# Moving the split activation u by 96 bytes in SBUF in a two-block transformer kernel

## The reference, cut to what matters

```python
def modulate(x, g, shift, scale):
    return rmsnorm(x, g) * (1 + scale) + shift
x = x + 0.5 * m[:, 2] * swiglu(modulate(x, norm_g[i, 0], m[:, 0], m[:, 1]), w_gate, w_up, w_down)
...
h = rmsnorm_2(x, pre_norm[layer])
proj = h @ w_in[layer]
```

## Time and profile before

| | |
|---|---|
| time, median of 3 runs | 2276.56 us (2274.78 to 2280.75) |
| span of the profiled execution, first to last instruction (its own time; nothing around it is given) | 2276.9 us |
| TensorE (PE) matmuls busy | 2135.6 us, 94% |
| weight loads (PEld), beside the matmuls | 2025.3 us, 89% |
| VectorE (DVE) | 1453.4 us, 64% |
| ScalarE (ACT) | 963.4 us, 42% |
| mean granted TensorE clock | 0.941 of full |

### The profile page before, as it was taken

How to read it: one execution, slowest core, us unless ns; L and a number is a source line. 1 busy time by engine, 2 the same in 40 slices (tenths; PEclk the granted TensorE clock), 3 DMA queues, 4 the chain that set the end, 5 groups by cost and what they waited for, 6 DMA issues and landing times.

```text
span 2276.9 us, 38695 instructions
## 1 busy us (share of the span) xinstructions
PE 2135.6 (94%) x16399; PEld 2025.3 (89%) x16399; DVE 1453.4 (64%) x1820; ACT 963.4 (42%) x1091; POOL 174.4 (8%) x153
## 2 busy tenths in 40 slices
PE   5999999999979899999999999999998898899897
PEld 4999999987749799999999899999998698899767
DVE  3546777779789957777644644557755445775543
ACT  2433433334325644334333533445445345534532
POOL 1000000000010000000000000003300000330000
PEclk9999999999989799999999899999998889999878
DMA  9688688733233348886655355544434034443401
GB/s 322 241 276 277 222 275 295 269 105 119 74 93 121 107 143 278 277 293 224 208 186 180 109 188 186 182 133 149 131 113 130 8 123 145 138 127 112 130 1 56
DMA packets 270793, 383.86 MB, mean 169 GB/s; under 512 B 8441, under 2 KB 230727, under 8 KB 270679
## 3 DMA queue, kind: packets, MB, share of 16 engines
q1 hardware_dynamic: 246983, 293.59, 40.1%
q0 software_dynamic: 22288, 85.02, 10.7%
q10 hardware_dynamic: 1408, 3.59, 0.4%
HBM read 381.06 MB, written 1.11 MB: 168 GB/s over the span
## 4 chain that ended last, share of the span: by engine, by line
PE 80%; DVE 13%; ACT 4%; issue 3%; DMA 0%; SPq 0%; DVEq 0%; ACTq 0%
PE bank L635 21%; PE bank L636 21%; PE bank L637 21%; PE bank L1081 3%; DVE w_hl L1764 3%; PE bank L661 2%; ACT w_hl L1319 1%; DVE e_long L2143 1%; DVE e_long L2161 1%; PE bank L696 1%; DVE conv_acc L2092 1%; PE bank L681 1%; PE bank L708 1%; PE bank L1128 1%; ACT p_tile L1660 1%
## 5 line engine op out<-in xcount | busy, mean ns | idle before, releaser
L1764 DVE TENSOR_TENSOR w_hl<-raw,w_hl 128x2048 fp32r<-128x2048 f32 (+1 forms) x281 | 641.7, 2284 | 434.5 <-ACT w_hl L1319 434.2
L1319 ACT ACTIVATE w_hl<-raw 128x2048 fp32r<-128x2048 f32 (+1 forms) x281 | 532.3, 1894 | 223.7 <-PE bank L637 218.9
L635 PE MATMUL bank<-u_hl,w_hl 128*128 128x256 f32 x2080 | 596.1, 287 | 0.0
L636 PE MATMUL bank<-u_hl,w_hl 128*128 128x256 f32 x2080 | 591.9, 285 | 0.0
L637 PE MATMUL bank<-u_hl,w_hl 128*128 128x256 f32 x2080 | 591.7, 284 | 0.0
L635 PEld LDWEIGHTS bank<-u_hl,w_hl 128*128 128x128 f32 x2080 | 402.6, 194 | 10.1 <-issue 8.4
L636 PEld LDWEIGHTS bank<-u_hl,w_hl 128*128 128x128 f32 x2080 | 402.6, 194 | 0.0
L637 PEld LDWEIGHTS bank<-u_hl,w_hl 128*128 128x128 f32 x2080 | 402.4, 193 | 0.0
L635 PE MATMUL bank<-h_hi,w_hl 128*128 128x256 f32 x800 | 226.8, 284 | 3.8 <-DVE h_lo L1861 3.8
L636 PE MATMUL bank<-h_lo,w_hl 128*128 128x256 f32 x800 | 225.8, 282 | 0.0
L637 PE MATMUL bank<-h_hi,w_hl 128*128 128x256 f32 x800 | 225.5, 282 | 0.0
(11 more groups left out here) (395 smaller groups left out, 4108.2 us busy)
## 6 DMA issues: line engine op xcount, KB each, us to landing
ada<-in_ada_w POOLq DMA_DIRECT2D x72, 1024.0 KB, 7.0
raw<-in_w_in SPq DMA_DIRECT2D x60, 1024.0 KB, 5.2
raw<-in_ffn_w_gate SPq DMA_DIRECT2D x55, 1024.0 KB, 7.2
raw<-in_ffn_w_up SPq DMA_DIRECT2D x55, 1024.0 KB, 5.3
raw<-in_ffn_w_down SPq DMA_DIRECT2D x55, 1024.0 KB, 5.0
raw<-in_ssd_w_in SPq DMA_DIRECT2D x20, 1024.0 KB, 5.3
raw<-in_w_out SPq DMA_DIRECT2D x16, 1024.0 KB, 5.2
raw<-in_ssd_w_out SPq DMA_DIRECT2D x8, 1024.0 KB, 5.1
```

The source lines that it names most:

```text
L635: pe.matmul(out_, wh, xh, start=start, stop=False, skip_group_check=True)
L636: pe.matmul(out_, wh, xl, start=False, stop=False, skip_group_check=True)
L1319: nc.scalar.activation(whi[slot][:, 0:n], raw[slot][:, 0:n], ACT.Copy).then_inc(S["hi_done"], 1)
L1764: ve.tensor_tensor(wlo[slot][:, 0:n], raw[slot][:, 0:n], whi[slot][:, 0:n].bitcast(F32), ALU.subtract)\
```

## The change

`u_hl` begins 96 bytes later, at byte 98,528, which is 96 past a multiple of 128 (and 224 past one of 256). A further 32 bytes behind it make the whole shift 128 bytes for all that follows: `scratch` is on a multiple of 128 as before, `region` is 136,416, still 96 past a multiple of 128. What overlays u (`ada[6]`, `ada[7]`, `fin_hi`, `streams`) takes its address from `u_at` and moves by 96 too; the second half of `streams` is worked out from `region` and stays on `uc_hl`. No instruction is added, removed or moved.

```diff
         x = fixed("x", [P, KB, T])
+        top[0] += 96
         u_at = top[0]
         u_hl = fixed("u_hl", [P, 2, KB, T], F32R)
+        top[0] += 32
         u_hi, u_lo = u_hl[:, 0, :, :], u_hl[:, 1, :, :]
         scratch_at = top[0]
         scratch = fixed("scratch", [P, KB, T])
```

## The result

The change made the kernel slower: 2286.11 us (median of 6 runs, 2282.93 to 2288.83) against 2276.53 us (6 runs), 9.6 us or 0.42% by the medians; the ratio over the runs is 1.003 with a 95% interval of 1.0016 to 1.0045. The profiled run took 2286.14 us, 1.6 us more than its span. Forecast were 2266.0 us and a range from 2262.5 to 2277.0.

What follows compares the result with a forecast made beforehand. The prediction took TensorE's distance between matmul starts to bound the kernel; 10.0 + 0.3 + 0.5 + 0.4 + 0.2 - 0.2 - 0.6 = 10.6 us off 2276.6 gave 2266.0 us, range 2262.5 to 2277.

Steps and rivals of the forecast that it cites:

- What bounds the kernel: FFN stages with u moving: TensorE never idles, so stage time is matmul count times the distance between two starts.
- The distance and what it goes with: Matmul starts: 120.0 ns with u_hl, 118.2 with uc_hl; weights and moving operand collide at one place of a 128-byte period.
- The rule of the Trainium skill that was weighed: TensorE: independent read ports, 256 columns an estimated 109 ns wherever the operand lies; addresses are nothing, time stays.
- u moving through the triplets: ffn1 to ffn4 and the two big projections: 6240 matmuls go from 120.0 to 118.4 ns, gaining 10.0 us.
- wrong in the period if ffn0 or h lengthens: Sign in the profile after: longer ffn0 or h distances, expected to stay at 118.2 to 118.4 ns, would refute the period.
- shift by 128 or not at all: zero, from both sides, unless 256 counts: ScalarE's hi part, x, scratch and the rest: their shift costs and gains zero, unless a period of 256 counts.
- the period is 256, and the new place is bad: Rival: h, uc_hl and g lose 1.6 ns each, 2283.0 us, or u's worse place gives 2295; chance 0.05 for either.
- 512 columns: 504 matmuls of 512 columns, one half moving off the multiple: gain 0 to 0.8 us, 0.4 taken.
- u stationary: 624 matmuls with w moving and u loaded: gain 1.6 ns each, 1.0 us, or nothing; 0.5 us taken.
- The lo writes of u: VectorE's 64 writes of u's lo part beside norms: 476 ns becomes 483, 0.2 us lost.
- The rival of the region of SBUF: Rival: SBUF region, not low address bits, sets the distance; u keeps 120.0 ns, 2276.6 us, no change; chance 0.13.
- The rival in which half of the gain is given back: Rival: u stationary, 512 columns and output projection give nothing, second-block mixer waits take 3.5 us; 2270.2 us, chance 0.13.

Runs made afterwards that it cites:

- w_128: Kernel before with only the split weights w_hl moved, by 128 bytes, and the activations kept in place modulo 256: ratio 1.0019, 2284.86 us.
- u_224: Kernel before with u beginning 224 bytes later and everything behind it 256 bytes later: ratio 0.9949, 2266.68 us.
- u192_rest192: Kernel before with all moving activations placed 192 bytes past the weights modulo 256: ratio 0.9863, 2245.28 us.
- rest_only_128: Kernel before with u in its old place and everything behind it moved by 128 bytes: ratio 1.0042.

## Why the prediction was wrong

**What bounds the kernel** was right: the distance between starts decides in these stages, and the sum of distances times counts, +9.5 us, lies in the measured interval of 3.6 to 10.2.

**The distance and what it goes with** was right in kind: the low address bits of the weights and of the moving operand matter, and w_128 shows that it is their relation. That two streams of reads collide is a reading of this which no run tests by itself. The second stream could be the writes of w_hl by VectorE and ScalarE, which share its address bits. Against it speaks the trace of before: for about a microsecond in the projection neither has an instruction, and the matmuls keep their 0.12 us.

```profile
1500.37 2.29 DVE L1764 TENSOR_TENSOR w_hl<-raw,w_hl 128x2048 fp32r<-128x2048 f32 x1 [1.41 <-ACT w_hl L1319]
...
1502.78 0.28 PE L635 MATMUL bank<-u_hl,w_hl 128*128 128x256 f32 x1
...
1503.62 0.28 PE L636 MATMUL bank<-u_hl,w_hl 128*128 128x256 f32 x1
...
1503.70 0.60 ACT L1606 ACTIVATE hgrn_k<-bank 128x512 f32<-128x512 f32 x1 [3.36 <-PE bank L637]
```

(7 matmuls in 0.84 us.) Over the whole trace of before, u moving has 119.8 ns in the 669 distances during which VectorE, ScalarE and GpSimd are all idle, and 119.8 in the 3947 during which w_hl is written; for uc_hl the two are 118.2 (105) and 118.3 (700). The 1.6 ns are there without the writes. A pattern begun under writes could still be carried into these stretches, so the writes are unlikely and not excluded. The DMA's writes into `raw` are out: `raw` kept its place against uc_hl in w_128, and uc_hl changed all the same.

The rule of the Trainium skill that was weighed, two independent read ports of TensorE ("TensorE: Matmul & The Clock Gate", Step-by-step: what each phase is for), doesn't describe this stream: distances from 113.3 to 120.0 ns at one granted clock, with nothing changed but addresses. The 262 cycles for 256 columns that the prediction took from the same page stand there for an isolated gap and not for a stream with weight loads, so 109 ns was a weaker rival than it looked.

**The step that failed** is in the part "u moving through the triplets", and under it the sentence that the change puts u where uc_hl is "in that period". I took the period to be 128 bytes. Nothing in the trace said so: all places I compared were 128 and 96 past a multiple of 256, and that fits either. With 256, u's new place was one that no row had shown, and the gain of 10.0 us was never there; u moving cost 1.0 us more. u_224 is the kernel that the working described: there u moving runs at 118.4 ns. That its time of 2266.68 us stands so close to the forecast 2266.0 is partly luck, since the kernel before ran 2 us slower beside it. The prediction's own sign, "wrong in the period if ffn0 or h lengthens", came true: both went from 118.4 to 120.0 ns.

**"shift by 128 or not at all: zero, from both sides, unless 256 counts"** failed with it: the shift of the rest made the loss, 6.5 us of it in uc_hl, h and g. The rival "the period is 256, and the new place is bad" named this mechanism with this price, 2283.0, and had 0.05. It left out the 512 columns (+2.1) and the output projection (+1.0), and those with u (+1.0, and -1.1 stationary) make the rest up to 9.5. The two readings of the period had the same support in the rows, and I gave 0.64 to the one and 0.05 to each of the two bad ends of the other.

**Smaller terms.** u stationary was right in sign and larger, 2.1 ns where 1.6 was the upper bound. 512 columns went the other way: D = 0 for u's half and 224 for the context's gave 229, 96 for both gave 233, and 224 for both also 233. The lo writes of u in their new place:

```profile
L1805 DVE SCALAR_TENSOR_TENSOR u_hl<-scratch,mods,u_hl x40: 472/474/485, 57.8 to 1301.5; 128x256 fp32r<-128x256 f32 x40
```

474 ns against 476 in the earlier trace rows, not 483: zero where 0.2 us stood. The rival of the region of SBUF is out, since u gained in its own region (u_224). In u_224 no gain was given back that its interval could show; in u192_rest192, whose distances gain 44.8 us, some was.

Three slips in the working changed nothing. The rival in which half of the gain is given back adds up to 6.0 us and not 6.4; the 13.5 us at the favourable end give 2263.1 and not 2264; and the trace has 72 lo writes onto u's bytes (the 40 shown, 16 to `streams` and 16 in the second block), not 64.

## What to carry to other kernels

Where TensorE is never idle and its weights and moving operand are both read from SBUF, compare the distance between matmul starts across tensors that differ only in address, and map the start of one against the other in 32-byte steps; here it was worth 1.4% with no instruction changed. Measure each placement whole: here the price at one D wasn't the same in every stage and every mixture. Before a pad goes in, list everything behind it: a pad moves all that follows, and the part that nobody named can carry the cost. And when a pattern is read from residues, name every period that the places seen can't tell apart, and give each its chance.

## What was not expected of the hardware

- The distance between starts of 256-column float32r matmuls with their weight loads took stage means from 113.3 to 120.0 ns at a granted clock of 1.00, with nothing changed but start addresses. For u moving the stage means at D = 0, 96, 128 and 224 stayed within 0.5 ns of each other, at 32 within 0.7, at 64 and 160 within 1.4 (the two projections taken one by one), and at 192 they lay up to 4.4 apart.
- At one pair of addresses two steady patterns exist, 113.3 and 117.8 ns, each kept over many chunks.
- Two moving operands that alone have 119.8 (D = 0) and 120.0 ns (D = 96) had 117.8 when mixed (the output projection in rest_only_128).
- 512 columns in two halves took 228.6 to 230.5 ns or 233 to 233.5 ns. With the distances of u and of uc_hl: 229.1 at (0, 224), 230.0 at (0, 96), 230.5 at (96, 224), 228.6 at (32, 64), 229.1 at (64, 64), 230.1 at (160, 192), but 233 to 233.5 at (96, 96), (224, 224), (128, 96), (32, 192), (192, 192) and (192, 64). I found no rule in it.
